# S5 lag products and the last operator transposes, one projection tile later in TensorE's order

## The reference

```python
h, gt, gtc = _prologue(x, ctx, c, c_ctx, norm_g, w_mod, b_mod)      # RMSNorm, scale, shift
u, v, g_a, xs, g_b = jnp.split(h @ w_in, [...], axis=-1)            # each 512 wide
y_a = _chunk_gmlp(u, v, gm_v_g, gm_w_s, gm_b_s) * jax.nn.silu(g_a)  # layer norm of v, 128x128 mixing
y_b = _s5_bidir(xs, n_ctx, lam_re, ..., w_glu, b_glu) * jax.nn.silu(g_b)
x = x + gt * (jnp.concatenate([y_a, y_b], -1)[:, n_ctx:] @ w_out)
# _s5_bidir: forward and backward diagonal state-space scans over xs, 32 groups of
# 16 channels and 64 states; y = fwd + bwd + d_skip * xs
```

## Time and profile before

| | |
|---|---|
| median of 3 runs | 1206.2 us (1206.08 to 1206.79) |
| profiled execution, device time | 1204.7 us |
| its span | 1202.9 us |
| TensorE matmul busy | 1151.2 us (96%) |
| TensorE weight load busy | 952.1 us (79%) |
| VectorE busy | 827.4 us (69%) |
| ScalarE busy | 499.2 us (41%) |
| GpSimd busy | 428.3 us (36%) |
| chain that ended last | TensorE 80%, VectorE 12%, DMA 4%, ScalarE 2% |
| mean granted TensorE clock | 0.993 of full |

### The profile page before, as it was taken

The page is one execution under the profiler, slowest core; times in us unless marked ns, Lnnn a source line. Parts: engine busy times, 40 slices in busy tenths (PEclk is TensorE's granted clock), DMA queues, the critical chain, the costliest instruction groups (busy, mean ns, idle before and its releaser), DMA issues.

```text
span 1202.9 us, 16681 instructions
## 1 busy us (share of the span) xinstructions
PE 1151.2 (96%) x6482; PEld 952.1 (79%) x6482; DVE 827.4 (69%) x1264; ACT 499.2 (41%) x932; POOL 428.3 (36%) x336
## 2 busy tenths in 40 slices
PE   2899899999999999999999999999999999999996
PEld 2678789887888987878888888877777777777885
DVE  5699949899926365037839978249888888884237
ACT  3444556210014642134523432246666666664012
POOL 4810000000000002442211113148888888887232
PEclk9999999999999999999999999999999999999998
DMA  9933885435421936213021122330000000000403
GB/s 340 365 115 125 212 259 203 143 113 180 159 88 58 329 139 232 70 50 130 31 70 36 36 79 80 98 111 9 10 18 10 18 19 10 19 10 27 161 23 131
DMA packets 81022, 129.81 MB, mean 108 GB/s; under 512 B 12944, under 2 KB 43024, under 8 KB 80144
## 3 DMA queue, kind: packets, MB, share of 16 engines
q1 hardware_dynamic: 71120, 113.96, 28.1%
q10 hardware_dynamic: 9824, 14.80, 3.5%
HBM read 97.81 MB, written 30.93 MB: 107 GB/s over the span
## 4 chain that ended last, share of the span: by engine, by line
PE 80%; DVE 12%; DMA 4%; ACT 2%; issue 1%; POOL 1%; ACTq 0%; DVEq 0%; SPq 0%
PE ps L1869 9%; PE ps L1871 9%; PE ps L1870 9%; PE ps L1880 5%; PE ps L1881 5%; PE ps L1882 5%; DVE region_d L1125 3%; PE ps L2153 3%; PE ps L2183 3%; PE ps L2182 3%; PE ps L2181 3%; PE ps L2231 2%; PE ps L2233 2%; PE ps L1734 2%; PE ps L2232 2%; PE ps L2202 2%
## 5 line engine op out<-in xcount | busy, mean ns | idle before, releaser
L1869 PE MATMUL ps<-w_hi,a_hi 128*128 128x512 f32 x448 | 176.9, 395 | 5.7 <-DVE b_lo L1213 4.4
L1870 PE MATMUL ps<-w_lo,a_hi 128*128 128x512 f32 x448 | 175.0, 391 | 0.0
L687 POOL TENSOR_TENSOR region_b<-region_b,region_d 128x512 f32<-128x512 f32 x20 | 26.3, 1328 | 404.5 <-DVE region_d L1525 404.5
L1871 PE MATMUL ps<-w_hi,c_lo 128*128 128x512 f32 x368 | 143.3, 389 | 0.0
L1880 PE MATMUL ps<-a_hi,w_hi 128*128 128x512 f32 (+1 forms) x384 | 138.0, 359 | 0.0
L1881 PE MATMUL ps<-b_lo,w_hi 128*128 128x512 f32 (+1 forms) x384 | 136.0, 354 | 0.0
L1882 PE MATMUL ps<-a_hi,w_lo 128*128 128x512 f32 (+1 forms) x384 | 135.9, 354 | 0.0
L680 POOL TENSOR_TENSOR w_lo<-weight_ring,w_hi 128x2048 fp32r<-128x2048 f32 x14 | 65.1, 4653 | 185.5 <-ACT w_hi L736 185.5
L1619 DVE TENSOR_REDUCE small<-ps 128x1 f32<-128x1280 f32 x64 | 95.0, 1484 | 40.1 <-PE ps L2153 40.1
L709 POOL TENSOR_TENSOR region_c<-region_c 128x512 f32<-128x512 f32 x80 | 109.7, 1372 | 28.3 <-ACT region_c L1096 25.3
L1869 PEld LDWEIGHTS ps<-w_hi,a_hi 128*128 128x128 f32 x448 | 84.6, 189 | 25.5 <-issue 6.5
(11 more groups left out here) (253 smaller groups left out, 2683.2 us busy)
## 6 DMA issues: line engine op xcount, KB each, us to landing
weight_ring<-in_w_mod SPq DMA_DIRECT2D x10, 2048.0 KB, 9.0
weight_ring<-in_we_in SPq DMA_DIRECT2D x10, 1024.0 KB, 5.7
weight_ring<-in_wo_in SPq DMA_DIRECT2D x10, 1024.0 KB, 5.1
weight_ring<-cop_t_scratch SPq DMA_DIRECT2D x4, 1536.0 KB, 8.5
region_c<-in_w_mod SPq DMA_DIRECT2D x2, 2048.0 KB, 21.5
bop_scratch<-region_d ACTq DMA_DIRECT2D x16, 256.0 KB, 2.5
cop_t_scratch<-region_d SPq DMA_DIRECT2D x8, 512.0 KB, 7.0
weight_ring<-bop_scratch SPq DMA_DIRECT2D x2, 2048.0 KB, 10.4
```

The source lines that it names most:

```text
L1869: te.matmul(o, th, wh[:, k % 4], start=k == 0, stop=False)
L1870: te.matmul(o, th, wl[:, k % 4], start=False, stop=False)
L1871: last = te.matmul(o, tl, wh[:, k % 4], start=False, stop=k == KT - 1)
```

## The change

Three entries of the table `after_xs` move: `("lags", 0)` from behind tile 1 to behind tile 2, `("lags", 1)` from behind tile 6 to behind tile 7 (where it stands ahead of `("gb", 0)`), and `("bop", 12)` from behind tile 7 to behind tile 8 (ahead of `("vg", 0)`). Since TensorE and ScalarE both walk this table, the order of both changes. VectorE's, GpSimd's and SyncE's lists are the same, and no instruction is added or removed.

```diff
@@ -358,8 +358,8 @@
-        after_xs = {0: [("vs", 0)], 1: [("lags", 0), ("xs", 1)], 2: [("vs", 5)], 3: [("bop", 8)], 4: [("ws", 0)], 6: [("lags", 1), ("vr", 0)],
-                    7: [("gb", 0), ("bop", 12)], 8: [("vg", 0)], 9: [("vg", 5)]}
+        after_xs = {0: [("vs", 0)], 1: [("xs", 1)], 2: [("lags", 0), ("vs", 5)], 3: [("bop", 8)], 4: [("ws", 0)], 6: [("vr", 0)],
+                    7: [("lags", 1), ("gb", 0)], 8: [("bop", 12), ("vg", 0)], 9: [("vg", 5)]}
```

## The result

The changed kernel takes 1209.6 us (median of 8 runs, 1208.0 to 1211.2), the kernel before 1206.1 us in the same session (8 runs, 1205.6 to 1206.8): a ratio of 1.0027, with a 95% interval of 1.0018 to 1.0036. It is 3.4 us slower, where 1.5 us were forecast. TensorE's mean granted clock is 0.989 instead of 0.993, and its matmuls are busy for 1155.6 us instead of 1151.2: the same matmuls took 4.4 us longer, which no wait explains.

The account below looks back on a forecast made before the run. TensorE, 96% busy, bounds the kernel; DMA sets the pace from 176 to 198 us. Saved waits of 1.58 + 3.25 us, less 2.2 at `bop` 8 and later losses, give +1.5: 1207.7 us, range 1205.6 to 1209.8.

Parts of the forecast that it names:

- within 0.2%: Whole kernel: a result told as the same, 0.2% being 2.4 us; chance 0.71.
- No wait ahead of the lags: TensorE, projection: the waits of 1.58 and 3.25 us ahead of the two lag groups go.
- 2.2 us at `bop` 8, starting near 127.7: TensorE, `bop` 8 transposes: a new wait of about 2.2 us for ScalarE's `region_d` copies, starting near 127.7.
- Tile 9 near 158.7, tile 11 ending at 172.8: TensorE, end of the projection: tile 9 starts at 158.7 instead of 161.73, tile 11 ends at 172.8 instead of 175.7.
- `u_in(2)` near 176.5 with tile 11's copy right behind it: ScalarE: issue waits for the store of tiles 6 to 8; TensorE waits some 4.5 us ahead of the mixing stage.
- The far case of a landing 2 us later: `bop` 12 store 2 us later: TensorE reaches the second half +2.3 us late, +3.5 if the last store is as late.
- First load of `bop_scratch` near 175.4 by SyncE's own list: SyncE: issued when the second `kt_out`'s issues end at 175.4, not at tile 11's end; lands at 186.1, no wait.
- TensorE waits for the second load, landing near 199.7: L1952, second half: TensorE arrives at 198.6, the second `bop_scratch` load lands at 199.7, so it starts 1.5 us late.
- The last term of the sum: Store of tiles 9 to 11: about 1.5 us later, so the second load and L1952's second half are +1.5 us.
- Gain kept: Rival: store of tiles 6 to 8 lands by 172.8, L1952's second half starts 3.0 us early, 1203.2 us; chance 0.07.
- Slower by the first load holding back the store of tiles 9 to 11: Rival: store lands at 191.4 (case begins past 188.4), second load at 202.1, 1210.1 us; chance 0.22 with late mixing stage.
- if in (6) the store waited for the first load: Sign of being wrong, at the wait for the second load: the store of tiles 9 to 11 waits for the first.

Follow-up runs that it names:

- a4: The changed kernel again, unchanged, as a control: 1210.3 us, ratio 1.0036 to the kernel before.
- d1: The kernel before again, unchanged, as a control: 1206.3 us, ratio 0.9997.
- a2: The kernel before with only lags 0 moved behind tile 2: 1204.0 us, ratio 0.9985.
- c1: The kernel before with lags 0 behind tile 2 and `bop` 8 behind tile 4: 1206.2 us, ratio 1.0002.
- b2: The changed kernel with ScalarE's copies and stores of `bop` 12 behind the store of tiles 6 to 8: 1207.3 us, ratio 1.0014 to the kernel before.
- b3: The changed kernel with the edits of b1 and b2 together: 1205.1 us, ratio 0.9989 to the kernel before.
- a3: The kernel before with only lags 1 and `bop` 12 moved: 1208.0 us, ratio 1.0018.
- b1: The changed kernel with `bop` 8 one tile later, behind tile 4: 1206.3 us, ratio 1.0001 to the kernel before.
- c3: The changed kernel with the edits of c2 and b1 together: 1204.3 us, ratio 0.9989 to the kernel before.
- c2: The changed kernel with four stages instead of two for `bop` 12: 1207.4 us, ratio 1.0011 to the kernel before.
- a1: The changed kernel with `u_in(2)` issued behind the copy of tile 11: 1207.9 us, ratio 1.0008 to the kernel before.
- b4: The changed kernel with the second `kt_out` held until the first two `bop` 12 stores have landed: 1210.9 us, ratio 1.0037 to the kernel before.

## Why the prediction was right in its mechanism and short in its size

The sign and the place were right: the waits go from the lag products to ScalarE's list, and the net is a small loss. The last step, that the second load then sets the end, did not come. The time, 1209.6, is 1.9 us above the 1207.7 forecast, inside the range and close to its end; "within 0.2%", which had 0.71, was missed by about 1 us. That the time lies in the range at all is in part luck. The end of the range was worked out for a late last store, which didn't come, and what filled the room, the clock, was in no term. And the forecast was worked out from the profile of before, against which the profiled loss is 5.9 us of span and not 1.5; the medians are only 3.4 apart since the first profile of before lies 1.5 below its median and that of the changed kernel 1.0 above.

1. **No wait ahead of the lags**: right, in every profile with that order.
2. **2.2 us at `bop` 8, starting near 127.7**: 2.19 us, ending at 127.57.
3. **Tile 9 near 158.7, tile 11 ending at 172.8**: right in its working, but 1.6 us were missing. In the first profile tile 9 starts at 160.37 and tile 11 ends at 174.40, and the slower clock behind `bop` 8 alone cost 1.6. In a4, where the clock did not fall, the `bop` 8 transposes start 0.8 us later than forecast (128.53), and tile 11 ends at 173.7 (179.52 less 5.81), 0.9 later than forecast: the working holds.
4. **`u_in(2)` near 176.5 with tile 11's copy right behind it**: right in kind, 179.81 in size. Of the 3.3 us, 1.6 are the clock again. The rest is the term that failed: "that run had stores that landed in about 2.0 us" was carried over to the new place, with 2.5 us for the second store only. The first took 4.4 and the second 4.0, and the four went out in 6.20 us, 2.4 more than assumed; the two loads behind them were issued 0.9 us quicker. The far case of a landing 2 us later, which the bounds did hold, is what came.
5. **First load of `bop_scratch` near 175.4 by SyncE's own list**: 176.28, right behind the last `kt_out` store.
6. **TensorE waits for the second load, landing near 199.7**: the load was issued at 189.8 and landed 9.4 us later, near 199.2, but nobody waited. The store of tiles 9 to 11 landed at 189.7, where the sum had 189.0. TensorE got to the second half of L1952 only at about 203.8 (194.40 + 9.37). The last term of the sum, +1.5 us by way of the store of tiles 9 to 11, was hidden behind a mixing stage that was 5.2 us later than the 189.2 worked out.

What the sum lacked is the clock. It took every matmul at its duration before, and so took idle time for idle time. The first profile's 4.1 us between the forecast end of L1952 (199.7 + 9.0 = 208.7) and the 212.8 measured come out as 1.6 for the clock behind `bop` 8, 1.7 for ScalarE's list (3.3 less 1.6), 1.9 for the clock in the mixing stage, less the 1.1 us of wait for the second load that didn't come. These terms are read off one profile and not measured one by one.

**The rivals.** Gain kept: refuted, the store of tiles 6 to 8 took 10.0 us, within 0.3 us of its 9.7 before, and not the estimated 3.5. Slower by the first load holding back the store of tiles 9 to 11: its time did not come, but its mechanism did, and the prediction's own sign of being wrong, "if in (6) the store waited for the first load", is there. The first load landed at 186.5 us. `u_in(2)`, issued 3.5 us behind it, took 7.9 us (4.2 before, where it was issued ahead of the load) and landed 1.3 us after the load; the store landed at 189.7, 3.2 us after it. So it is in every profile. In the eight with `u_in(2)` issued behind the load, the store lands 2.7 to 3.5 us after the load has landed, in the six with it ahead (before, d1, a2, c1, b2, b3) 1.7 to 1.8 us, whenever it was issued. What the rival had wrong is the price, 5.3 us behind the load instead of 3.2; the forecast's +1.5 for `u_in(2)` running behind the load is what the profiles show. It decided nothing, as TensorE itself was later. The limit of 188.4 at which this case was to begin was a slip: in the forecast's own sum the store lands at 189.0 (199.7 less the load's 10.7), which is past it. The loss beyond 2.4 us, which had 0.22, came by what the rival calls "a late mixing stage", and by the clock.

**Which part costs what**, by the ratios: lags 0 alone -0.15% (a2), lags 1 and `bop` 12 alone +0.18% (a3), together +0.27% (+0.36% in a4). They don't add: alone, lags 0 turns a short and a long wait into two of like size, and hardly anything behind them moves (the mixing stage starts 0.3 us earlier, and L1952 ends 1.0 us earlier); together, the time won at lags 0 is already lost at `bop` 8, and the rest is lost on ScalarE. Taking the wait at `bop` 8 out is worth 3.3, 2.3 and 3.1 us by the medians, 2.7 to 3.1 by the ratios, in the changed order (b1 against the changed kernel, b3 against b2, c3 against c2) and costs 2.2 in the old one (c1 against a2). In the changed order nothing between `bop` 8 and the mixing stage holds the gain back, since ScalarE's list moves forward too; in the old one lags 1 wait for VectorE's `CL` at 146.5 whatever came before, so that the time is given back there, in one long piece.

**What stays open.** Why the clock falls behind 2.19 us of idle time in after, a1, b2, b4 and c2, and not in a2 and a4. Whether the packet of code delays the store, which all eight traces fit and no run isolates. And that before mostly pays for the slower clock rests on two profiles of it; the mean clock that each timed run gives is too coarse to part them.

## What to carry to other kernels

A wait that is taken away pays only where the engine's next wait doesn't take the time back; follow the in-order list of every engine that issues DMAs down to the next stage before counting it, since one wait for a landing (`u_in(2)`) ahead of a copy that TensorE needs decides more than the order of the matmuls. Count idle time of TensorE by its pieces and not by its sum: here two pieces of 2.1 and 2.2 us cost nothing beside themselves in the one profile of a2, and one of 4.5 us cost some 1.3 us more up to the mixing stage. And where a two-buffer stage waits for stores to land, don't carry a best landing time over to a new place: two more buffers took about 2 us off at once.

## What the hardware did that I had not expected

Granted clock: with idle times of 4.0 to 7.0 us ahead of the mixing stage it fell to 1.2 GHz every time (nine profiles), always before the idle time had ended, and the stage took 13.3 to 13.8 us by the chain (180.94 to 194.56 in the changed kernel) instead of 11.7 (a2); at 4.50 and 3.25 us ahead of lags 1 it fell in two profiles of three; at 2.2 us ahead of `bop` 8 in five of seven, each time 0.9 to 1.4 us after TensorE had started again, for 1.6 us in the one worked out above; at 2.36 us ahead of the mixing stage once (a1), at 2.10 (a2), 1.58 and 0.78 never.

Landing: the first store of `bop` 12, 256 KB on ScalarE's queue, landed in 2.0 us in the four profiles with `bop` 12 at its old place and in 3.7 to 4.4 us in eight with it at the new one, in one of them with nothing from SyncE's queue beside it (b4). Only the last of its 16 completions was late, and a 16 KB packet of program code was on the DMA engines in the eight, and in none of the four.

Two queues: the last store to `xs_scratch`, 640 KB on ScalarE's queue, landed 1.7 to 3.5 us after SyncE's 2 MB load had, in all fourteen profiles, though it was issued from 0.6 us to 5.7 us behind that load. When it lands is told better by the end of the load than by its own issue.
